# Three-pass output projection, a reordered first group and joins by half rows in a two-layer RWKV-7 and attention kernel

## The reference: what is computed

```python
# layer 0: RWKV-7 time mix, then SwiGLU
h = rms_norm(x, norm_g); dx = shift(h) - h
xr, xw, xk, xv, xa, xg = (h + dx * mu[i] for i in range(6))
r, k, v = xr @ w_r, xk @ w_k, xv @ w_v
w = -softplus(-(w0 + tanh(xw @ w1) @ w2)) - 0.5       # decay
a = sigmoid(a0 + (xa @ a1) @ a2); g = sigmoid(xg @ g1) @ g2
kk = normalise(k * k_k); k = k * (1 + (a - 1) * k_a)
o = wkv7_scan(r, exp(-exp(w)), k, v, -kk, kk * a)      # by heads of 64
x = x + ((group_norm(o) + bonus) * g) @ w_o
x = x + (silu(gate) * up) @ w_down
# shared K/V of x, then layer 1: dilated attention, three groups, 16 heads of 64
q = rope(rms_norm((rms_norm(x) @ w_q)))
o = merge over groups of softmax(q k^T / 8 + mask) v
x = x + o @ b_w_o                                      # 256x1024 times 1024x1024
x = x + (silu(gate) * up) @ w_down
```

## Time and profile before

| | |
|---|---|
| median of 3 runs | 996.15 us (995.2 to 996.47) |
| profiled execution: time, span | 994.96 us, 993.2 us |
| PE busy | 956.9 us, 96% of the span |
| DVE busy | 671.4 us, 68% |
| ACT busy | 432.4 us, 44% |
| granted clock, mean | 0.998 |
| start and first mixes | 0 to 28 us |
| four RWKV groups | 28 to 292 us |
| join and feed-forward 0 | 292 to 487 us |
| join and eight passes of the heads | 487 to 767 us |
| output projection, its join | 767 to 811 us |
| feed-forward 1 | 811 to 993 us |

### The profile page before, as it was taken

One profiled execution on the slowest core, in us unless ns is written; L12 is line 12 of the kernel. 1 busy time (PEld: TensorE's weight loads), 2 busy tenths in 40 slices (PEclk: granted clock), 3 DMA queues, 4 the chain that ended last, 5 costly groups with the idle time before them and its releaser, 6 DMA issues.

```text
span 993.2 us, 17418 instructions
## 1 busy us (share of the span) xinstructions
PE 956.9 (96%) x6660; PEld 818.3 (82%) x6660; DVE 671.4 (68%) x1234; ACT 432.4 (44%) x687; POOL 83.2 (8%) x66
## 2 busy tenths in 40 slices
PE   5989999999999999999989999999999999999998
PEld 4868678687788888888888999999999478888887
DVE  6873955747757666666577878787877357666665
ACT  3312313113225444444345565656665444444442
POOL 0111000000010000000011221122212000000000
PEclk9999999999999999999999999999999999999999
DMA  9310320500513766666458455545555036666661
GB/s 302 129 56 2 121 63 1 170 14 18 153 43 105 214 190 190 189 191 190 125 192 233 118 160 149 146 116 161 150 144 151 14 103 198 188 189 191 190 190 59
DMA packets 195124, 136.83 MB, mean 138 GB/s; under 512 B 7278, under 2 KB 185966, under 8 KB 194940
## 3 DMA queue, kind: packets, MB, share of 16 engines
q1 hardware_dynamic: 195068, 136.03, 46.7%
HBM read 134.96 MB, written 1.05 MB: 137 GB/s over the span
## 4 chain that ended last, share of the span: by engine, by line
PE 83%; DVE 10%; issue 4%; ACT 1%; DMA 1%; POOL 1%; SPq 0%; POOLq 0%; DVEq 0%; ACTq 0%
PE bank L415 45%; PE wide L415 35%; DVE work L1193 2%; DVE work L1190 2%; DVE work L1424 1%; DVE x L1190 1%; DVE work L1416 1%; PE wide L844 1%; DVE work L1408 1%; PE bank L844 1%; ACT work L906 1%; PE wide L823 1%; POOL gsm L1653 1%; DMA x<-in_x 0%; DMA ring<-in_w_kv 0%
## 5 line engine op out<-in xcount | busy, mean ns | idle before, releaser
L415 PE MATMUL bank<-wpj,hkq 128*128 128x384 f32 x1152 | 215.3, 341 | 3.5 <-DVE hkq L1190 3.5
L415 PEld LDWEIGHTS bank<-wpj,hkq 128*128 128x128 f32 x1152 | 199.0, 189 | 7.1 <-issue 5.4
L415 PE MATMUL wide<-hsp,wsp 128*128 128x256 f32 (+2 forms) x1120 | 193.9, 329 | 0.9 <-DVE hsp L1190 0.9
L415 PEld LDWEIGHTS wide<-hsp,wsp 128*128 128x128 f32 x1120 | 172.4, 190 | 24.1 <-DVE hsp L1190 1.3
L1190 DVE TENSOR_TENSOR wsp<-ring,wsp 128x1024 fp32r<-128x1024 f32 (+1 forms) x88 | 150.7, 1752 | 4.2 <-ACT wsp L906 4.2
L906 ACT ACTIVATE wsp<-ring 128x1024 fp32r<-128x1024 f32 (+1 forms) x88 | 130.3, 1485 | 21.7 <-PE wide L415 14.0
L1190 DVE TENSOR_TENSOR wpj<-ring,wpj 128x1536 fp32r<-128x1536 f32 x48 | 84.2, 1754 | 21.2 <-ACT wpj L906 21.2
L415 PE MATMUL bank<-wsp,asp 128*128 128x512 f32 x396 | 98.1, 392 | 0.0
L1653 POOL TENSOR_TENSOR gsm<-gsm,mhalf 128x6 f32<-128x6 f32 (+1 forms) x40 | 61.7, 1575 | 308.4 <-DVE gsm L1592 215.5
L906 ACT ACTIVATE wpj<-ring 128x1536 fp32r<-128x1536 f32 x48 | 71.2, 1484 | 32.3 <-PE bank L415 26.1
L415 PEld LDWEIGHTS bank<-wsp,asp 128*128 128x128 f32 x396 | 71.7, 189 | 13.1
(11 more groups left out here) (174 smaller groups left out, 1106.2 us busy)
## 6 DMA issues: line engine op xcount, KB each, us to landing
ring<-in_f_w_gu SPq DMA_DIRECT2D x88, 512.0 KB, 5.8
ring<-in_w_kv SPq DMA_DIRECT2D x96, 256.0 KB, 3.6
ring<-in_f_w_down SPq DMA_DIRECT2D x44, 512.0 KB, 3.7
ring<-in_b_w_q SPq DMA_DIRECT2D x48, 256.0 KB, 3.6
wmix<-in_a_w_k SPq DMA_DIRECT2D x4, 1024.0 KB, 7.4
wmix<-in_a_w_r SPq DMA_DIRECT2D x4, 1024.0 KB, 10.1
wmix<-in_a_w_v SPq DMA_DIRECT2D x4, 1024.0 KB, 5.3
wmix<-in_a_w_o SPq DMA_DIRECT2D x4, 1024.0 KB, 5.1
```

Source lines behind the costliest of these rows:

```text
L415: return pe.matmul(o, a, b, start=start, stop=stop)
```

## The change

The diff, cut to its core (memory names that only make room are left out; no new function is called that is not here).

```diff
 # output projection, PE (product_out) and its operands
-        oT = sbv("oT", [P, KT, T])
+        oT = ctx.enter_context(nc.sbuf_tensor("oT", [P, KT, T], F32R))     # and oT_lo, wo_e, wo_g, wo_r, wo_h
+        EARLY_PIECES = {2: 0, 3: 1, 4: 2, 5: 3}
+        WO_PIECES = ((0, 0, wo_g[:, :]), (0, 2, wo_r[:, :]), (0, 4, wo_h[:, :]), (0, 5, wo_e[:, :]), (0, 6, hkq[:, 1, 0, 1024:2048]),
+                     (1, 0, slot0[:, 0:1024]), (1, 2, slot0[:, 1024:2048]), (1, 4, slot0[:, 2048:3072]), (1, 6, slot1[:, 0:1024]))
-                    m = mm(bank[...], oT[:, k, ...], wo_v[:, k, ...], k == 0, k == KT - 1)
+                    pe.wait_ge(S("dve_wo_lo"), piece + 1)
+                    mm(o, oT[:, k, cut], high, k == 0, False)
+                    mm(o, oT_lo[:, k, cut], high, False, False)
+                    m = mm(o, oT[:, k, cut], wmix_low[:, k, j * 512:(j + 1) * 512], False, k == KT - 1)
 # ACT heads(): high parts of b_w_o
+                if X and not follow: wo_high(4, last + 8)        # ahead of half_hi(7, 5)
+                if X and not follow: wo_high(5, last + 10); wo_high(6, last + 10)   # behind copy_o(1)
+                if X and p in EARLY_PIECES: wo_high(EARLY_PIECES[p])    # ahead of half_hi(p + 1, 1)
+                if X and not follow: wo_high(7, last + 10); wo_high(8, last + 12)   # at the end of pass 7
 # DVE heads(): low parts of b_w_o and of the attention's output
+                if not X: wo_low(5)        # ahead of normalise(0)
+                if not X: wo_low(6)        # ahead of normalise(1)
+                if not X: wo_low(7); wo_low(8); out_lo(0); out_lo(1)
-                if X and follow: half_lo(p + 1, 0); half_lo(p + 1, 1)
+                if X and follow: half_lo(p + 1, 0)
+                if X and B: out_lo(0); out_lo(1)
+                if X and follow: half_lo(p + 1, 1)
+                if X and p in EARLY_PIECES: wo_low(EARLY_PIECES[p])
+                if X and not follow: wo_low(4)
 # SP: the second down load of ffn(1) now also waits
+                elif layer > 0 and b == 1:
+                    sp.wait_ge(S("pe_awo"), 3)
 # PE, last scores: the blocks are cut otherwise
-                    weigh(0); product_out(0, 1, range(4)); turn_p(1); product_out(0, 1, range(4, 7)); weigh(1)
+                    product_out(0, 1, range(2)); weigh(0); turn_p(1); product_out(0, 1, range(2, 4)); weigh(1); product_out(0, 1, range(4, 7))
 # ffn(1), PE: rows 1 are turned ahead of the low products of tile 0
+                    turn_half_rows(2 * RT, 1)
                     ... low_weights(0, m_, slice(0, P))
-                    turn_half_rows(2 * RT, 1)
-                    keep_clock(4, 1)
 # start and first group, PE
+                keep_clock((1, 10)[r], 4)                 # behind turning rows r of hn
+            project(7, 1, xk, "pe_k", [0]); second_rank(0); project(7, 1, xk, "pe_k", (1, 2, 3))
+                    project(4, 0, xr, "pe_r", [0]); sums_of_squares(); project(4, 0, xr, "pe_r", (1, 2, 3))
-                early = EARLY if behind else 4
+                early = EARLY                              # group 0 too fills level 1 with two value quarters
 # first group, DVE: group_columns(0) (pg) moves ahead of the first turned rows; mix(3, xv) moves from
 # ahead of the group to behind t1; then kT_, clamp, reciprocal, kn, bb, kP, first half of ar,
 # receptances (rkr, second half of ar), bP. ACT: the root stands ahead of the three exponentials.
 # POOL: the 4096-column memset follows the last mix, which is now xv
 # SP: wa2 and g2s of group 0 are loaded ahead of the constants
 # RWKV to ffn(0), PE
-            keep_clock(8, 4); turn_output(NGRP, [1], 3); keep_clock(7, 4); product_o(NGRP, [1], 1); keep_clock(2, 4)
-                    turn_half_rows(0, 0); keep_clock(6, 6)
+            keep_clock(1, 4); turn_output(NGRP, [1], 3); keep_clock(6, 4); product_o(NGRP, [1], 1, [0])
+            turn_half_rows(0, 0); product_o(NGRP, [1], 1, [1])
 # and DVE: rows_lo(0) stands between add_output 2 and 3
 # ffn(0) to heads, DVE
-                half_lo(0, 0) ahead of the four additions into x
+                    if i == 3 and layer == 0: mean_row(1, 0)
+            scale_half(1, 0, 0, ...); mean_row(1, 1); scale_half(1, 0, 1, ...); scale_half(1, 1, 0, ...)
+            rows_lo(K, [0]); scale_half(1, 1, 1, ...); rows_lo(K, [2]); half_lo(0, 0); rows_lo(K, (1, 3))
+            scale_rows(ahn2, 0); half_lo(0, 1); scale_rows(ahn2, 1); rows_lo(Q, (0, 1, 2, 3)); half_lo(0, 2)
 # ACT: half_hi(0,0), squares by 512 columns, rows_hi(K), half_hi(0,1), rows_hi(Q), half_hi(0,2)
 # PE
-            keep_clock(22, 4); turn rows 0; keep_clock(6, 4); turn rows 1
+            keep_clock(6, 4); turn (0,0), (0,1), two more, (1,0), (1,1), two more
-                        pe.wait_ge(S("dve_aturned"), 4 * what + 4)
+                        pe.wait_ge(S("dve_aturned"), 2 if u == 0 else 4 * what + 4)
-                    project_half(1); turn_queries(1)
+                    project_half(1, [0]); turn_queries(1); project_half(1, [1])
 # PE scores(0) waits for dve_oT instead of act_oT
```

More of the change, by code:

```diff
@@ L1380, in group, with receptances, guard_squares @@
                 step(m)
+                arf = ar.rearrange("p n c m t -> p (n c) m t")
+                def receptances():
+                    dve.wait_ge(S("pe_r"), it + 1)
+                    for n in range(2):
+                        m = stt(rkr[:, n, :], bank[4][:, n * T:(n + 1) * T], pgc(n, "r_k"), kT_[:, n, :], ALU.mult, ALU.mult)
+                    m.then_inc(S("dve_rkr"), 1)
+                    tt(arf[:, :, 1, :], v4(bank[4]), E1[:, :, 1:129], ALU.mult)
+                def guard_squares():
+                    dve.wait_ge(S("pe_ss"), it + 1)
+                    dve.tensor_scalar(rn, bank[3], 1e-24, None, ALU.max).then_inc(S("dve_ssm"), 1)
+                if not behind:
+                    mix(3, xv, "dve_mix")
                 dve.wait_ge(S("pe_k"), it + 1)
```

290 lines of the change are left out of this document (179 added, 111 removed).

## The result

| | median | lowest to highest | runs |
|---|---|---|---|
| before | 996.31 us | 995.2 to 997.48 | 4 |
| after | 980.14 us | 978.93 to 981.88 | 4 |

The ratio is 0.9839, with a 95% interval of 0.982 to 0.9858: 16.2 us faster. The profiled execution of after is the slowest of its four: 981.88 us, span 980.1, against 994.96 and 993.2 before. So the two traces lie 13.1 us apart, and the medians 16.2. That gap has to be explained too.

What follows compares the result with a forecast made beforehand. PE's own work was taken to bound the long loops, so only four places could gain: 3.1 + 1.7 + 4.5 + 6.6 = 15.9 us off the profiled 994.96 gives 979.1, plus 1.2 for the median: 980.3; 8 in 10 between 975.5 and 986.

Steps and rivals of the forecast that it cites:

- first group: Start up to the matrices and doubling levels: new order gains 3.9, clock 1.4, less the fill; 3.1 us in all.
- RWKV to feed-forward: Join ahead of feed-forward 0: fewer identities and earlier turned rows bring the second tile's high products 1.7 us forward.
- feed-forward to heads: Join behind feed-forward 0: earlier first projection and third half bring pass 1 forward; 4.5 us, ends 3.1 and 6.4.
- last scores to feed-forward 1: Output projection in three-pass products, smaller pieces and reordered rows: rows 1 of feed-forward 1 start 6.6 us earlier.
- everything of the first group behind them moves by 1.4: First group: identities keep TensorE at its upper clock, small products end 1.4 us earlier and later work follows.
- The fill: First doubling level of the first group: two value quarters moved in there cost 2.2 us, at most 3.2.
- Memset against DVE: Rival, first group: key product, clamp and reciprocal stand still beside POOL's memset, 2.3 us lost, 982.6; chance 0.09.
- pass 1 starts 4.1 to 5.0 us earlier: Second join: with the load moved 3.1 to 4.1 us, copy and V behind it, pass 1 starts that much earlier.
- the load (0.10): Rival, second join: the 4 MB load and the half behind it keep their place; join gives 1.5, 983.3; chance 0.10.
- the short stay at the lower level (0.05): Rival, second join around 490: idle PE briefly drops TensorE to 1.2 GHz, costing 2.2 us, 982.5; chance 0.05.
- three passes save nothing: Rival, output projection: ACT and DVE splitting nine pieces set the pace, the 5.3 us go, 985.6; chance 0.06.
- The other side: Slower case: TensorE falls to 1.2 GHz at the second join and the first pass runs there, 17 slower, 1013; chance 0.02.

Runs made afterwards that it cites:

- e_hold: Changed kernel plus nineteen identity products filling TensorE's three waits at the end of pass 0, load left in place (also called the hold): 978.83 us.
- e_direct: Changed kernel with only the output projection's three-pass product undone, each step one direct product of unsplit f32 values again: 984.00 us.
- h_four: e_hold with the first projection of the heads waiting again for all four split quarters of the turned rows, not only two: 983.63 us.
- the spread load: Changed kernel with the one 4 MB load of b_w_o split into eight 512 KB loads behind weight halves of pass 1: 976.57 us.
- e_nowarm: Changed kernel without the 1 and 10 identity products behind the first turned rows: 980.86 us.
- the faster version: Changed kernel with b_w_o in eight loads, fifth high piece behind the last weight half, last turned queries inside pass 1's first high products: 973.82 us.
- h_nowarm: e_hold without the 1 and 10 identity products behind the first turned rows: 978.77 us.

## Why the prediction held, step by step

The forecast was 980.3 us and the result 980.14, inside the range. The four places in the traces, each by how much farther ahead of before the next fixed row stands than the last:

| place | predicted | traces |
|---|---|---|
| first group, from PE's first row to the second group's matrices | 3.1 | 3.3 |
| RWKV to feed-forward | 1.7 | 2.0 |
| feed-forward to heads | 4.5 | 2.6 (5.6 with the clock held and the load 0.8 sooner) |
| passes, last scores to feed-forward 1 | 6.6 | 6.1 |
| later first load, as PE's first row shows it | | -0.8 |
| sum | 15.9 | 13.2 |

The first and the fifth row belong together: the second group's matrices stand at 113.32 for 115.86, which is 2.5, and 2.9 against the traces with an earlier first row (112.98 to 113.00).

The traces give 13.2 (13.1 by the spans) and the medians 16.2. The gap is the profiled executions: that of after is 1.7 above its median, and that of before 1.4 below its own. The hold shows that after's executions differ at the second join, by the clock and by the landing of the load. Before's differ with the clock as well: of its nine runs in the second session the two with a mean clock of 0.998 took 994.8 and 995.21 us, the seven with 0.993 to 0.996 from 995.96 to 997.7.

So the hit within 0.2 us is partly luck. The median of after lies 14.8 under before's profiled execution, where the sum of the steps was 15.9. The forecast meets it because it added 1.2 for the median of before, which is a matter of before's clock and need not carry over to a new kernel; in after the difference of profiled execution and median has the other sign.

**First group.** The sum held (2.5 to 2.9 for 3.1), its parts partly by luck. I gave 3.9 to the order and 1.4 to the clock. From the first row to the matrices it is 46.78 us before, 41.34 after and 42.54 in the execution of after's order without identities that had the same long slow stay as before: 4.2 for the order, 1.2 for the clock, in an execution with the long stay. Counted from DVE's first mix, which starts alike in the two without identities (13.52 before, 13.50), the order gave 3.8, and the 3.9 was right. But by the medians the identities are worth 0.06. The step that failed is "everything of the first group behind them moves by 1.4": what a short stay costs, 0.56 up to the keys, the identities cost too, because they let DVE's first mix start later. The fill costs 2.17 (2.2 taken).

**Memset against DVE.** Refuted where I had put it, and the reason was right: key product, clamp and reciprocal don't stand still (0.68, 0.69, 3.35). The mechanism is real for a copy, at 2.96 us for four columns. The operands that I read in the GPSIMD Engine Reference of the Trainium skill (table, SBUF interfaces) sort them the right way round here; which interface holds the copy no run shows.

**RWKV to feed-forward.** 2.0 for 1.7; PE's wait ahead of rows 1 is 1.32, I had 1.6.

**Feed-forward to heads.** The head of it came as costed: the first projection 5.8 us nearer to the last sums was forecast, the trace has 6.1 (10.63 ahead, less 4.54), and the third half 7.2 instead of 6.4. The step that failed is the end: "pass 1 starts 4.1 to 5.0 us earlier". I had seen that the load comes late and took its wait of 2.75 as a sign, but not as the limit that it would be. The load was issued 3.4 us earlier by this join, inside my 3.1 to 4.1 (502.73 for 510.70, less 4.54), so pass 1 could not come 4.1 to 5.0 earlier once it waited for the load. ACT's half landed 6.8 us ahead of its old time (522.53 for 529.32), of which this join has 2.3, because the way from the issue to ACT took 19.8 us and not 18.6; the work around it came 7.2 ahead. Then the clock took 2.3 more, against 1.3 in before. So two of my rivals were at work here, the load (0.10) and the short stay at the lower level (0.05). I looked for the latter at 490, where PE's waits of 0.67 and less did no harm, and not at the wait that the load makes. With the clock held the join is worth 5.6, and the median of after lies 1.3 above that kernel, which leaves 4.3 for the 4.5. That this comes so near is luck, since neither the late load nor the fallen clock was in the 4.5; and what the median execution looks like at this join no trace shows.

**The passes.** 33.17 us up to pass 7, as costed; DVE's room covers the pieces.

**Last scores to feed-forward 1.** The high piece ahead of the weight half cost 0.94 (1.0 taken). From the product's start to feed-forward 1 it is 28.21 us instead of 33.04: 4.8, and I had 5.9. Undoing the three passes alone costs 4.0 there, with the new wait of 0.40 in it, so they are worth 4.4 of the 5.3 expected: the step is 0.697 us in the long rows, and the first product of each block starts 0.1 us late, which a sum of steps leaves out. The smaller blocks gave 0.85 (33.04 less 32.19), where I had 1.6; the new wait for the scaled rows 0 is 0.40, where I had 1.0. What follows gave 2.2 for 1.7, of which the order alone has 1.7. On the Trainium skill's 216 ns for 512 columns (TensorE: Matmul & The Clock Gate, Back-to-back issue gap), which that section gives as the gap of a single product: the row decided rightly, 0.232 here too. The rival that three passes save nothing is refuted by the direct version, 3.9 slower (its trace has a long stay at the lower level in front of pass 1 too, 6.85 us for the 24 products, so I go by the 4.0 of this stretch).

**The other side.** The clock did fall, but returned after 6.7 us in after's trace, and after 6.8 at the longest (h_four); no pass ran at the lower level.

## What to carry to other kernels

When you pull the work of a join forward, list the loads that queue between it and the next stage, and ask of each whether it moves too: a large load that isn't wanted until later belongs behind the small ones that are. Price a wait of TensorE of one and a half to three microseconds at more than itself, because the work behind it may run at half rate: here it did so for 3 to 7 us. And before reading a difference of one microsecond, take the source of scatter away: with nineteen identities the spread of the runs fell from 2.95 to 0.24 us. Then ask what else the filler does; here it also hid when the load landed, and each row that is used as a point to count from has to be tested for whether the work behind it really follows.

## What the runs showed of the hardware

- TensorE went to half its clock within idle times of 2.93 and 2.66 us with little work before them (after and h_four, 1.1 and 1.9 us into the wait), and also about waits of 1.65 us and less in a row (the spread load's profiled execution, 0.50 from 521.5 to 524.9; e_nowarm and e_direct, from 520.9 and 520.7). Of the traces of the new order the five with a wait of 1.64 us or more at this join all show it, with a stay of 3.4 to 6.8 us; of the runs not all do, since three of the spread load's five have a mean clock of 1.0. The 24 products behind it took 1.1 (e_nowarm) to 2.8 us (h_four) more than 4.40. The length of the stay doesn't follow the length of the wait: e_direct waited 1.64 and then 0.40 us, and its products took 6.85. With no wait over 0.67 us at this join the mean granted clock was 1.0 in all five runs of e_hold, and so it was in the five of the faster version, with a wait of 1.07 there.
- The granted clock in the records isn't always the rate of the work: in before and in h_nowarm's trace the slow products of 16 to 20 us stand beside a granted clock of 1.00, in e_nowarm's beside 0.50. In h_nowarm the execution with the long slow stay has a mean granted clock of 1.0, and the four faster ones, of which there is no trace, 0.998. So the length of the products is to be read beside the clock's column.
- A copy on DVE that is started beside a POOL memset lasts until the memset ends (3.55 us for 28 columns before, 2.96 for 4 columns here, which took 0.16 ahead of the memset), and holds what follows it; products out of PSUM, the clamp and the reciprocal beside the same memset aren't stretched.
- The 4 MB load and the weight half behind it land at times that vary by about two microseconds between executions of nearly the same program: from the issue of the 4 MB to ACT's first work on the half it is 17.5 (e_nowarm) to 19.8 us (after) in the twelve traces with the one load.
